# Seven RMS norms rebuilt: root with tokens on partitions, last square summed apart, constant products at the waits

## What is computed

```python
def rms_norm(x, g):
    xf = x.astype(jnp.float32)
    y = xf * lax.rsqrt(jnp.mean(xf * xf, axis=-1, keepdims=True) + EPS)
    return (y * g.astype(jnp.float32)).astype(x.dtype)
...
hx = rms_norm(x, norm1_g[layer]) * (1 + mod_x[1]) + mod_x[0]
...
x = x + mod_x[5] * sqrelu_mlp(rms_norm(x, norm2_g[layer]) * (1 + mod_x[4]) + mod_x[3], mlp_w1[layer], mlp_w2[layer])
```

## Time and profile before

| | |
|---|---|
| median of 3 runs | 2670.71 us (2670.26 to 2671.92) |
| the profiled execution | 2669.27 us, of which the span of the trace is 2667.5 |
| busy: PE, PEld | 2443.4 (92%), 1970.1 (74%) |
| busy: DVE, ACT, POOL | 1489.1 (56%), 972.6 (36%), 1141.5 (43%) |
| mean granted TensorE clock | 0.956 |

### The profile page before, as it was taken

The page is one execution under the profiler, slowest core; times in us unless marked ns, Lnnn a source line. Parts: engine busy times, 40 slices in busy tenths (PEclk is TensorE's granted clock), DMA queues, the critical chain, the costliest instruction groups (busy, mean ns, idle before and its releaser), DMA issues.

```text
span 2667.5 us, 31916 instructions
## 1 busy us (share of the span) xinstructions
PE 2443.4 (92%) x11638; PEld 1970.1 (74%) x11638; DVE 1489.1 (56%) x1987; ACT 972.6 (36%) x1519; POOL 1141.5 (43%) x857
## 2 busy tenths in 40 slices
PE   7999887999999988699989999797888889899999
PEld 6888776888888877466678888676644666688877
DVE  6856866737273745988452123479588443543433
ACT  4322334212121326577452233442434353432322
POOL 1533132535253522388544476344553331344444
PEclk6999998999999999799999999998999899999999
DMA  5433021424242321312222232132200110232323
GB/s 221 136 111 131 28 72 65 141 79 142 79 135 85 127 78 48 101 42 52 75 79 90 91 102 95 63 103 87 95 0 1 63 64 25 79 103 90 99 93 105
DMA packets 68822, 231.69 MB, mean 87 GB/s; under 512 B 8048, under 2 KB 10992, under 8 KB 68592
## 3 DMA queue, kind: packets, MB, share of 16 engines
q1 hardware_dynamic: 68720, 230.35, 26.7%
HBM read 219.57 MB, written 2.10 MB: 83 GB/s over the span
## 4 chain that ended last, share of the span: by engine, by line
PE 72%; DVE 11%; issue 8%; POOL 5%; ACT 3%; DMA 1%; SPq 0%; POOLq 0%; DVEq 0%; ACTq 0%
PE PS L676 53%; PE PS L694 8%; POOL HL L531 4%; PE PS L717 2%; DVE RD L2381 2%; PE PS L1152 1%; PE PS L976 1%; DVE ADJ L2013 1%; DVE SM L2365 1%; PE PS L1245 1%; PE PS L1141 1%; PE PS L751 0%; PE PS L1117 0%; PE PS L1160 0%; DMA EARLY<-adastream 0%
## 5 line engine op out<-in xcount | busy, mean ns | idle before, releaser
L531 POOL TENSOR_TENSOR HL<-RAW,HL 128x512 fp32r<-128x512 f32 x614 | 905.7, 1497 | 1316.8 <-ACT HL L1290 1316.5
L676 PE MATMUL PS<-HA,HL 128*128 128x512 f32 (+1 forms) x2592 | 556.9, 368 | 14.0 <-DVE VS L2484 4.6
L676 PE MATMUL PS<-HID,HL 128*128 128x512 f32 (+1 forms) x2832 | 565.6, 362 | 0.0
L676 PE MATMUL PS<-HB,HL 128*128 128x512 f32 (+1 forms) x2592 | 542.0, 361 | 0.0
L676 PEld LDWEIGHTS PS<-HID,HL 128*128 128x128 f32 x2832 | 478.8, 188 | 85.4
L676 PEld LDWEIGHTS PS<-HA,HL 128*128 128x128 f32 x2592 | 444.3, 190 | 106.8 <-issue 26.1
L676 PEld LDWEIGHTS PS<-HB,HL 128*128 128x128 f32 x2592 | 442.3, 188 | 77.1
L1290 ACT ACTIVATE HL<-RAW 128x1024 fp32r<-128x1024 f32 x307 | 323.1, 1053 | 475.0 <-PE PS L676 383.9
L2013 DVE CUSTOM_DVE_ANT_0 ADJ<-ADA,CB 128x1024 f32<-128x1024 f32 x160 | 269.1, 1682 | 9.2 <-DVE X L1935 2.7
L1935 DVE SCALAR_TENSOR_TENSOR X<-PS,MOD,X 128x256 f32<-128x256 f32 (+1 forms) x120 | 75.7, 658 | 334.7 <-PE PS L676 316.2
L694 PE MATMUL PS<-HA,HL 128*128 128x256 f32 (+1 forms) x576 | 138.7, 404 | 59.2 <-DVE HA L1916 44.0
(11 more groups left out here) (376 smaller groups left out, 2726.3 us busy)
## 6 DMA issues: line engine op xcount, KB each, us to landing
RAW<-wstream SPq DMA_DIRECT2D x307, 512.0 KB, 3.5
ADA<-adastream SPq DMA_DIRECT2D x80, 512.0 KB, 3.8
EARLY<-adastream SPq DMA_DIRECT2D x16, 512.0 KB, 14.5
QB<-QH SPq DMA_DIRECT2D x32, 128.0 KB, 2.3
X<-x_in SPq DMA_DIRECT2D x8, 384.0 KB, 6.4
QC<-QL SPq DMA_DIRECT2D x16, 128.0 KB, 2.3
out<-X SPq DMA_DIRECT2D x8, 256.0 KB, 2.3
X<-mem SPq DMA_DIRECT2D x1, 1024.0 KB, 5.6
```

What stands on the lines that cost most here:

```text
L531: a = pool.tensor_tensor(HL[:, t % RING, 1, half], RAW[:, t % RAW_RING, half], HL[:, t % RING, 0, half].bitcast(F32), ALU.subtract)
L676: mm = pe.matmul(bank(t % 2, r), w[:, wp, k * P:(k + 1) * P], a[:, ap, lo:hi], start=(k == 0 and (wp, ap) == (0, 0)), stop=(k == nk - 1 an ...
```

## The change

- The sum of squares is made with tokens on partitions: each block of 128 tokens of ACC is the stationary operand and one column of ones the moving one, so the sums are [128, number of blocks] in bank 5. Only seven squares are added into ACC; the last is multiplied by ones by itself and summed in the bank.
- Ln, Exp and the Newton step work on these few columns. `norm_spread` then puts the root back to all partitions, one 128-column product per block.
- VectorE scales X by gain and root in one instruction per region, from the bank, with the factor -0.5/D folded into the gains; ScalarE makes the high part alone (with the shift as bias); VectorE's low part adds the shift. Four buffers (T1 and T2) instead of two.
- `keep_clock` puts products of constants, whose result nobody reads, at TensorE's waits in each norm but 0a.
- The memory's norm: its squares move ahead of attention's output tiles, its root is made with that of 1b, its scale, high and low parts go into the last quarter of layer 1's MLP. 2a is of the image tokens alone.
- `ADA_PE` is 8 instead of 9. Modulation sums 46 and 47 move behind norm 0b; in layer 0's MLP the twelve of each quarter are spread 6 and 6 instead of 8 and 4. The wide products of 1a use banks 4 and 7 instead of 5 and 6.

```diff
@@ SyncE
-                    if j < 12:
+                    if j < 6:
                         ada(n_ada + j, q, 12)
+                    elif 8 <= j < 14:
+                        ada(n_ada + j - 2, q, 12)
@@ TensorE
-                pe.wait_ge(S("norm_acc"), of_norm(n, "acc", KC))
-                for r in regions:
-                    lo, hi = REG[r]
-                    mm = pe.matmul(PS[:, 5 if r == "c" else 6, 0:hi - lo], const(C_ONE), ACC[:, lo:hi],
+            def keep_clock(n, bk=4):
+
+                for _ in range(n):
+                    pe.matmul(PS[:, bk, 0:NCTX], const(C_ONE), CST[:, 0:2, :].rearrange("p n m -> p (n m)"), start=True, stop=True)
+
+            def norm_sum(n, regions, squares=None):
+
+                squares = squares or regions
+                blocks, last = blocks_of(regions), blocks_of(squares)
+                pe.wait_ge(S("norm_acc"), of_norm(n, "acc", KC - (n != "0a")))
+                for b in blocks:
+                    mm = pe.matmul(PS[:, 5, b:b + 1], ACC[:, b * P:(b + 1) * P], const(C_ONE)[:, 0:1], start=(b == blocks[0]),
+                              stop=True, skip_group_check=(b != blocks[0]))
+                if n != "0a":
+                    keep_clock(2 if len(blocks) > 4 else 1)
+                    pe.wait_ge(S("norm_sq"), of_norm(n, "sq", KC))
+                for b in last if n != "0a" else ():
+                    mm = pe.matmul(PS[:, 5, b:b + 1], SQ[:, (KC - 1) % 2, b * P:(b + 1) * P], const(C_ONE)[:, 0:1],
+                                   start=False, stop=True, skip_group_check=True)
+                mm.then_inc(S("norm_sum"), 1)
+
+            def norm_spread(n, regions):
+
+                if n != "0a":
+                    keep_clock(2)
+                pe.wait_ge(S("norm_root"), of_norm(n, "root", 1))
+                for b in blocks_of(regions):
+                    bk, o = (5, b) if b < NCTX // P else (6, b - NCTX // P)
+                    mm = pe.matmul(PS[:, bk, o * P:(o + 1) * P], RS[:, b:b + 1].to_broadcast([P, P]), const(C_ID),
                                    start=True, stop=True)
                 mm.then_inc(S("norm_sum"), 1)
+                if n != "0a":
+                    keep_clock(6 if n in ("0b", "1a") else 4)
...
-                norm_sum(nid, regions)
+                rows = "cx" if layer else regions
+                norm_sum(nid, rows, regions)
+                norm_spread(nid, rows)
@@ ScalarE
+                        if layer and isinstance(q, int):
+                            norm_high("2m", j, "c", None)
...
+            for k in range(KC):
+                square("2m", k, 0, NCTX, "mem_in", 16)
             for i in range(8):
                 tile(t)
                 square("1b", i, NCTX, NT, "x_new", of_norm("1a", "x_new", i + 1))
                 t += 1
+            norm_root("1b", "cx")
             norm("1b", "x", shift((1, 3)))
-            act.wait_ge(S("norm_hi"), of_norm("1b", "hi", KC))
-            for k in range(KC):
-                square("2m", k, 0, NCTX, "mem_in", 16)
-
-            act.wait_ge(S("norm_acc"), of_norm("2m", "acc", KC))
             mlp(1, t, "x", "2a")
@@ VectorE
+                link(dve.tensor_tensor(t, r, r, ALU.mult))
+                link(dve.scalar_tensor_tensor(t, PS[:, 5, b], D * EPS, t, ALU.add, ALU.mult))
+                dve.scalar_tensor_tensor(r, t, 3.0 * D, r, ALU.subtract, ALU.mult).then_inc(S("norm_root"), 1)
+
+            def norm_scale(n, k, regions):
+
+                if k >= 4:
+                    dve.wait_ge(S("norm_lo"), of_norm(n, "lo", k - 3))
+                for r in regions:
+                    lo, hi = REG[r]
+                    c = "xc".index(r)
+                    a = dve.scalar_tensor_tensor(norm_buffer(k)[:, lo:hi], X[:, k, lo:hi], AT[:, k, c:c + 1],
+                                                 PS[:, 5 if r == "c" else 6, 0:hi - lo], ALU.mult, ALU.mult)
+                a.then_inc(S("norm_scaled"), 1)
...
                 for k in range(KC):
-                    if k >= 2:
-                        dve.wait_ge(S("norm_hi"), of_norm(n, "hi", k - 1))
-                        scaled(n, k, lo, hi)
+                    norm_scale(n, k, regions)
                     if k:
-                        low(k - 1)
-                low(KC - 1)
+                        norm_low(n, k - 1, regions, bias)
+                norm_low(n, KC - 1, regions, bias)
...
                 for m in range(KC):
+                    if m:
+                        acc_square(next_norm, m - 1, lo, hi)
                     dve.wait_ge(S("tile_done"), t + m + 1)
                     residual(t + m, m, regions, gate).then_inc(S("x_new"), 1)
                     dve.wait_ge(S("x_new"), of_norm(stage, "x_new", m + 1))
                     dve.sem_inc(S("free_V"), 1)
-                    if m:
-                        acc_square(next_norm, m - 1, lo, hi)
-                    if next_norm == "0b":
+                    if next_norm == "0b" and m < 6:
                         ada(40 + m)
-                acc_square(next_norm, KC - 1, lo, hi)
...
-                        if layer == 0:
+                        if layer == 0 and j < 6:
                             ada(48 + j, q, 12)
+                        if layer and isinstance(q, int):
+                            norm_scale("2m", j, "c")
+                            if j:
+                                norm_low("2m", j - 1, "c", None)
...
+            gains(0, 4, PC["n2g"])
+            norm_root("0b", "cx")
+            norm("0b", "cx", shift((0, 3)))
+            for i in (46, 47):
+                ada(i)
             modulation(0, 40, ADA_CHUNKS)
-            gains(0, 4, PC["n2g"])
-            norm("0b", "cx")
```

More of the change, by code:

```diff
@@ L194, in span, with count, norm_buffer, blocks_of @@
             return REG[regions[0]][0], REG[regions[-1]][1]
-        NORMS = ["0a", "0b", "1a", "1b", "2a", "2b", "2c"]
         def of_norm(n, step, value):
-            order = [x for y in NORMS for x in ((y,) if y != "2a" or step not in ("sq", "acc") else ("2m", y))]
-            each = {"sum": 1, "rsqrt": 2}.get(step, KC)
-            return order.index(n) * each + value
+            order = ["0a", "0b", "1a", "1b", "2a", "2b", "2c"]
+            if step in ("sq", "acc"):
+                order.insert(3, "2m")
+            elif step in ("scaled", "hi", "lo"):
+                order.insert(4, "2m")
+            def count(x):
+                if step == "acc" and x not in ("0a", "2m"):
+                    return KC - 1
+                return {"sum": 2, "rsqrt": 2, "root": 1}.get(step, KC)
+            return sum(count(x) for x in order[:order.index(n)]) + value
+        def norm_buffer(k):
+            return (T1 if k % 4 < 2 else T2)[:, k % 2]
+        def blocks_of(regions):
+            lo, hi = span(regions)
+            return range(lo // P, hi // P)
         per = {"T": 16, "A": 8, "V": 8}
@@ L1396, in _ @@
             act.wait_ge(S("dve_once"), ONCE["first_gains"])
-            norm("0a", "cx", shift((0, 0)), root=False, between=lambda: high(2))
+            norm("0a", "cx", shift((0, 0)), between=lambda: high(2))
             t = 0
@@ L1908, in norm @@
-            def norm(n, regions, root=True):
-                lo, hi = span(regions)
-                if root:
-                    norm_root(n, regions)
-                def low(k):
-                    dve.wait_ge(S("norm_hi"), of_norm(n, "hi", k + 1))
-                    dve.tensor_tensor(H(k)[:, 1, lo:hi], T2[:, k % 2, lo:hi],
-                                      H(k)[:, 0, lo:hi].bitcast(F32), ALU.subtract).then_inc(S("norm_lo"), 1)
+                blocks = blocks_of(regions)
+                b = slice(blocks[0], blocks[-1] + 1)
@@ L1927, in residual, with shift @@
+            def shift(layer):
+                return lambda k, c: MOD[:, layer[0], layer[1] * KC + k, c:c + 1]
             def residual(t, m, regions, gate):
@@ L1976, in quarter @@
                         dve.wait_ge(S("free_V"), q * 8 + free0 + m + 1)
-                        if layer == 0 and m < 4:
-                            ada(56 + m, q, 12)
+                        if layer == 0 and m < 6:
+                            ada(54 + m, q, 12)
                         if layer == 0 and m == 7:
@@ L2103, in _ @@
             dve.sem_inc(S("dve_once"), 1)
-            norm("0a", "cx", root=False)
+            norm("0a", "cx", shift((0, 0)))
             dve.memset(V1[:, :, :, ML_DV:ML_DV + 1], 1.0).then_inc(S("dve_once"), 1)
@@ L2311, in _ @@
             gains(1, 1, PC["n1g"] + KC)
-            norm("1a", "cx")
+            norm_root("1a", "cx")
+            norm("1a", "cx", shift((1, 0)))
             dve.wait_ge(S("tile_done"), t + 2)
-            for i, bk in enumerate((0, 1, 2, 3, 5, 6)):
+            for i, bk in enumerate((0, 1, 2, 3, 4, 7)):
                 a = dve.tensor_copy(VA[:, i, :], PS[:, bk, 0:256])
@@ L2408, in _ @@
             att_low(ATT_HEADS // 2 - 1)
+            for k in range(KC):
```

(7 more changed lines are left out.)

103 lines of the change are left out of this document (58 added, 45 removed).

## The result

The changed kernel takes 2629.8 us, median of 4 runs (2627.3 to 2635.0), against 2671.3 of the kernel before (4 runs beside it, 2670.3 to 2672.3): ratio 0.985, interval [0.983, 0.987], 41.5 us less. The forecast was some 2635 (2635.4 by its sum). The profiled execution has a span of 2626.4 us (before 2667.5), 41.1 less; it is the one taken apart here.

What follows compares the result with a forecast made beforehand. It took TensorE's waits and slow stretches around six norms (gaps and pairs, 179 us) as the bound; 24.2 + 15.1 + 2.0 = 41.3, less 6 for the clock, gave 35.3 off 2670.7: 2635.4 us, eight in ten within 2618 to 2653.

Steps and rivals of the forecast that it cites:

- clock charge: In the norms' gaps: the granted clock falls in two of six, about 3 us each, 6 us added.
- six gaps: TensorE's stretches from last product before norms 0b to 2c to first after: shorter chain, 79.9 to 55.7 us.
- six pairs: First two weight tiles behind each gap: faster feed by VectorE, 99.2 to 84.1 us, 15.1 less.
- norm 0a: At norm 0a: fewer modulation chunks on TensorE, small products added, a sum dropped, faster feed; together 2 us less.
- moved work, layer 0's MLP: Modulation sums 46 and 47 behind norm 0b delay weight loads in layer 0's MLP: costs nothing, at small slack.
- memory's norm in layer 1's last quarter: Memory's scale, high and low parts moved there: 2.5 us more per tile fit, so no cost.
- The 0.7 us the forecast added for the feed: In pairs 1b and 2a: VectorE's 1.47 us a chunk against TensorE's 1.4, giving 11.9 us.
- Modulation sums 46 and 47 [...] Nothing, at small slack: In layer 0's MLP: weight loads wait some 25 us in, tile needed at about 35, so no cost.
- clock held in all: Rival: full clock kept in all six norms, 2629.4 us; chance 0.30.
- likeliest case: Clock falls in one to four norms: 2632 to 2641, forecast 2635, own range 2630 to 2642; chance 0.43.
- Pairs don't shrink: Rival: gaps shrink, but VectorE's feed takes 1.75 us a chunk, all 15 us of pairs lost: 2650; chance 0.08.
- the slower rival: Rival: clock falls and stays at half beyond the pair, deciding from 82 us, some 12 a norm; chance 0.02.

Runs made afterwards that it cites:

- the repeat: The changed kernel run once more, nothing altered, beside other runs on one chip, against the kernel before: 2621.2 us, ratio 0.985.
- the padded kernel: The changed kernel with 36 one-column products added at the start of TensorE's code, ratio against the kernel before: 2622.7 us, 0.985.

## Why the prediction held, step by step

The profiled execution is 41.1 us shorter, the forecast said 35.3 with a clock charge and 41.3 without. (Its new pairs add up to 83.9 and not 84.1, a slip of 0.2.) Its terms:

| | forecast | trace |
|---|---|---|
| six gaps (79.9) | 55.7, 24.2 less | 53.0, 26.9 less |
| six pairs | 15.1 less | 18.7 less |
| norm 0a | 2.0 less | 3.3 less |
| clock | 6 more | in the gaps' row: 1b, some 1.1 |
| moved work, layer 0's MLP | 0 | 6.5 more |
| memory's norm in layer 1's last quarter | 0 | 0.9 more |
| all else | 0 | 0.5 more |

- The gaps were right by their steps. Of the excess, 0.13 us for a spread instruction against 0.19 (from 128-column products elsewhere) gives 0.7 for six blocks. Gap 1b is the one long by its forecast (9.6 against 9.5), because its clock fell; 8.5 where it held.
- The pairs: VectorE is the feeder, 2.1 us a chunk in 0b (scale at 429.14 and 431.25) and not 2.2, so TensorE is no longer held up. In 1b and 2a it takes what an undisturbed pair takes, 11.2. The 0.7 us the forecast added for the feed wasn't there.
- The clock's charge of 6 was too dear. A fall in a gap costs 1 to 2.3 us, not 3, as the clock came back before the pair: 1.1 in 1b (against 8.5 in the repeat), 2.1 in 1a of the padded kernel. One or two falls in six is what most traces show, so the count was right and the price wrong. Which gap falls changes from run to run.
- **The step that failed** is "Modulation sums 46 and 47 [...] Nothing, at small slack" together with the silence on everything ahead of the loop: layer 0's MLP was costed at nothing and lost 6.5 us. No sum and no transfer was late; the constants and small products ahead of the loop pushed its body to a place where it doesn't stay loaded, and each turn of it waits for code. The memory's norm, the other moved part, was costed at nothing as well and costs 0.9, for VectorE is late with one low part.

The rival "clock held in all" (2629.4) matches the median to half a us, but not as a mechanism: savings were 7.6 us larger than forecast and the code's waits gave 6.5 of them back. The measured 2629.8 lies at the very edge of the likeliest case's 2630 to 2642. That it came so near is in part luck: the pairs and norm 0a gave more, the clock cost less, and a loss that nobody had forecast took most of it away. "Pairs don't shrink" is refuted by pairs of 11.2; the slower rival by pairs at clock 1.00.

The parts don't add. The norms without constants give 20 to 22 us, the constants alone 0 (perhaps 6 at a good place), both together 41. In the old pairs ScalarE's and VectorE's feed stood ahead of the clock; only when the feed is as fast as TensorE at full rate does the full rate show: the constants are worth 4.9 us in the gaps and 12.8 in the pairs of the new kernel, 3.2 and 5.7 in the old.

Open: the stretches of 672 products take 116.7 or 118.9 us at clock 1.00 in every kernel, by no pattern that I found; in layer 0's MLP alone it makes up to 9 us between two traces (four at 116.7 against four at 118.9). Why the wait grows by 0.1 to 2.3 us in most of the kernels and by 3.6 to 4.4 in one is seen only as far as one or two stops in a row; why a body that should fit by that estimate stays loaded at some places and is fetched anew in each turn, in eight or nine packets, at others isn't explained. No run takes the root with tokens on partitions, or the feed with one output of ScalarE, by itself; their shares are read from the timelines. Whether the changed kernel with its loop at a good place and no padding to pay for is faster than 2621 wasn't tried; by the stretches it would gain some 4 us.

## What to carry to other kernels

Cost a wait filler by what bounds the stretch behind it: keeping TensorE's clock up was worth nothing while another engine fed the chunks, and 18 us once the feed matched. When instructions are added ahead of a large loop, count the loop's place too: look at the packets of the instruction queue and at waits named "issue" at the loop's turns, before and after. Price small operations by the nearest row of the same shape on both sides, and price a clock fall only up to where the row shows it back.

## What the runs showed that was not expected

- A loop of 768 products on TensorE waits 1.24 us at its turn when its first product is the 1913th to 1935th of the code, up to 5.65 when it is the 1951st, and again 1.24 when it is the 1977th; six instruction packets against 32 to 34.
- A pair behind such a wait took 18.2 to 19.9 us instead of 16.9 where the wait had been over 2.5, but for one of 17.2 (memory's norm back in 2a); the clock was 0.91 and 0.84 in it where it was read: the stop brought a fall of the clock with it. Behind waits of 1.9 it took 16.9 in two traces and 18.7 in a third.
- One-column fp32 products: 0.12 us an instruction at full clock, 0.215 at half (15.5/72). A 256-column one: 0.28 at full (1.11/4) and 0.51 at half (2.05/4).
